# Block-by-block output projection, longer zero products, and a last expert whose result is added half by half, in an fp32 encoder kernel

## The chip, the cores and the metric

The kernel runs on one core of a Trainium2 chip. The metric is the device time in microseconds (us) of one execution; a median of several executions is given. Engines are called PE (TensorE, matrix products), DVE (VectorE), ACT (ScalarE), POOL (GpSimd) and SP (SyncE, which here only issues transfers). "bank" is a region of PSUM in which PE accumulates, 128 partitions by 512 numbers.

## The reference

Two layers over 256 tokens of width 1024, in float32: an even one and an odd one, each with a token mixer and a channel mixer.

```python
for i in range(DEPTH):                      # DEPTH = 2
    hn = rms_norm(h, norm_mix[i])
    if i % 2 == 0:  mix = fourier_mixer(hn, fourier_w_in[j], fourier_w_out[j])
    else:           mix = neighbourhood_attention(hn, nat_w_qkv[j], nat_rpb[j], nat_w_o[j])
    h = h + mix
    hn = rms_norm(h, norm_ffn[i])
    if i % 2 == 0:  ff = swiglu(hn, ffn_w_gate[j], ffn_w_up[j], ffn_w_down[j])
    else:           ff = moe_swiglu(hn, router_w[j], router_b[j], expert_w_gate[j], expert_w_up[j], expert_w_down[j])
    h = h + ff
return rms_norm(h, final_norm)
```

The Fourier mixer multiplies by `w_in`, takes the real part of a 2-D transform over tokens and over groups of 256 channels, and multiplies by `w_out`. `moe_swiglu` forms 8 logits for each token, sends the token to the two experts with the highest, weights their results by a softmax over the two, and adds. An expert is `(silu(x @ w_gate) * (x @ w_up)) @ w_down` with a hidden width of 3584. `rms_norm` multiplies by a gain vector per channel.

## The kernel before, in words

**Precision.** Every large product is three matmuls (`three`, L1250 to L1252): of each fp32 operand a high half `..._hi` (a rounding copy, made by ACT) and a rest `..._lo` (whole less high half, made by DVE) are kept, and high by high, high by low and low by high are added in one bank. Products of three that the profile names by these lines are all of this kind.

**Weights.** All weights come in pieces of 1 MiB (128 partitions by 2048 numbers, four 512-wide rows of one K tile each). SP loads them into seven slots `raw`; ACT makes `w_hi` (L458), DVE `w_lo` (L753), in three slots. `split_past(n)` in ACT's and in DVE's code makes all the pieces up to n + 3 that aren't made yet. PE's `ready` waits for a piece's `w_lo`; the last matmul on a piece frees its slot (`piece_used`). The very first weight piece is split in parts of 512 columns (L470, L761), and so is the second.

**Order.** No scheduler is at work: each engine's program is written out by hand, and an instruction that waits holds up all that stand behind it on its engine. The 256 tokens are two blocks b of 128, the 1024 channels two halves q (or c) of 512.

**Start.** PE first runs `still(12)`, twelve products of zeros (L1321, two trace records each), then `first_projection` (L1272: eight K tiles, each with its wait for a part of `w_lo`), the second half of `w_in`, and then `token_dft` and `channel_dft` for the Fourier mixer, in pairs of banks `T[m % 2]` and `Y[g % 2]`: product m waits until DVE is done with product m - 2 (`pt_lo_done`). `stream_second` (L1307) lets PE wait for `act_lo` of a new activation in two steps of two quarters.

**Output projection and router.** `wo_product(c, half, b)` multiplies by half of the attention's output matrix for column half c and token block b. DVE adds a result to h (`add_projection`, L797). PE transposes h (`transpose_stream(3, ...)`, L1297), ACT and DVE scale it by the norm's gain and halve it (L504, L778), PE multiplies with the router's weights `rw_parts` (`logits_hi` L1578, `logits_lo` L1585), and DVE finds the best two experts in a chain of small operations (L1013 to L1030, its result `used`). PE then ranks the tokens of each expert (L1610 to L1614), DVE makes a selection matrix `sel` (L1074), and PE gathers the first expert's tokens by products with it (L1619), transposes them (L1655) and starts the first expert. Between these waits PE runs `keep_warm(6)` and `keep_warm(2)`, products of an identity matrix that nobody reads (L1592; below they are called zero products too). `token_hi`, `token_lo` halve h for the gather. `split_past(W0 + n)` counts from the output projection's first piece; a piece is halved past it as soon as ACT and DVE come to that call.

**Experts.** For each expert PE runs, for seven steps c of 512 hidden columns, gate, up and, one step later, down (`down(c, half)`), the last one adding in the banks Y. The last expert, `LAST`, isn't handled by a loop: `result_hi` and `result_rest` halve its result, four pairs of products with `selT` (L1766, L1767) scatter it back to token order, and `add_result` (L1111) adds it to h. `gate_weights` (L1133) forms the two softmax weights, six small DVE operations in step 1 of that expert. ACT then squares the rows of h (L494), POOL makes 1/sqrt (L444, L446), DVE scales (L1236), and SP stores four parts of 256 KB (L392).

## Time and profile before

| | us |
|---|---|
| median of three executions | 1366.86 |
| lowest, highest | 1364.64, 1367.56 |
| the profiled execution | 1367.15 |
| its span in the trace | 1365.3 |

The span runs from the first to the last instruction in the trace; 1.85 us of the profiled execution lie outside it. The granted clock of PE was 0.992 on average. In the rows below, a line of the timeline gives start, duration, engine, source line, operation, result and operands, the number of records, and in square brackets how long the engine had been idle and what ended that. Consecutive matmuls overlap in the trace: the time of one is the distance of two starts, not its duration. A line of windows gives, for a stretch, its length, the busy time with the number of records, the granted clock (1.00 is full), the busy share of the transfer engines and GB/s.

### The profile page before, as it was taken

How to read it: one execution, taken by the hardware profiler on the slowest of the kernel's cores; microseconds unless marked ns; L12 is line 12 of the kernel's file. 1: busy time of each engine (PE TensorE's matmuls, PEld its weight loads, DVE VectorE, ACT ScalarE, POOL GpSimd, SP SyncE). 2: the span in 40 equal slices, each digit the busy share in tenths (PEclk: the TensorE clock that was granted, in tenths of full speed). 3: DMA queues.
4: the chain of work that ended last, by engine and by line, in shares of the span. 5: the costliest groups of instructions: out<-in, count | busy, mean ns of one | idle time of the engine just before them, and what ended most of it. 6: DMA issues, size and time to landing. Idle time of an engine off the chain costs nothing.

```text
span 1365.3 us, 17406 instructions
## 1 busy us (share of the span) xinstructions
PE 1344.7 (98%) x6341; PEld 1117.9 (82%) x6341; DVE 1111.9 (81%) x815; ACT 923.2 (68%) x755; POOL 34.5 (3%) x48
## 2 busy tenths in 40 slices
PE   8999999999999999999999999999999999999997
PEld 7888888787878888888888888888888888888885
DVE  5756666655678889888988988898898889889997
ACT  6554444545647778777777877877787787777774
POOL 0000000000101000000000000000000000002000
PEclk8999999999989999999999999999999999999999
DMA  9666775563339999999999999999999999999992
GB/s 354 246 207 179 210 211 190 175 204 104 101 109 378 383 378 365 395 382 357 398 388 372 373 394 377 358 398 388 368 376 394 367 370 397 381 374 385 396 394 90
DMA packets 194971, 432.32 MB, mean 317 GB/s; under 512 B 19632, under 2 KB 22064, under 8 KB 194800
## 3 DMA queue, kind: packets, MB, share of 16 engines
q1 hardware_dynamic: 178784, 416.28, 83.4%
q0 software_dynamic: 3360, 11.78, 2.2%
q10 hardware_dynamic: 12784, 3.69, 1.8%
q8 instruction: 27, 0.44, 0.1%
q14 instruction: 16, 0.13, 0.0%
HBM read 425.94 MB, written 5.78 MB: 316 GB/s over the span
## 4 chain that ended last, share of the span: by engine, by line
PE 95%; DVE 3%; ACT 1%; issue 1%; DMA 0%; POOL 0%; DVEq 0%; ACTq 0%
PE bank_G L1250 10%; PE bank_G L1252 10%; PE bank_G L1251 10%; PE bank_U L1250 10%; PE bank_U L1252 10%; PE bank_U L1251 10%; PE bank_Y L1250 8%; PE bank_Y L1252 8%; PE bank_Y L1251 8%; PE bank_T L1696 2%; PE bank_T L1250 1%; PE bank_T L1252 1%; PE bank_T L1251 1%; DVE w_lo L753 1%; PE bank_G L1512 0%
## 5 line engine op out<-in xcount | busy, mean ns | idle before, releaser
L753 DVE TENSOR_TENSOR w_lo<-raw,w_hi 128x2048 fp32r<-128x2048 f32 x390 | 885.9, 2289 | 184.6 <-ACT w_hi L458 183.8
L458 ACT ACTIVATE w_hi<-raw 128x2048 fp32r<-128x2048 f32 x390 | 748.6, 1920 | 276.6 <-PE bank_U L1252 98.2
L1250 PE MATMUL bank_Y<-w_hi,hidT_hi 128*128 128x512 f32 x492 | 192.2, 391 | 0.0
L1252 PE MATMUL bank_Y<-w_hi,hidT_lo 128*128 128x512 f32 x492 | 191.6, 389 | 0.0
L1251 PE MATMUL bank_Y<-w_lo,hidT_hi 128*128 128x512 f32 x492 | 191.5, 389 | 0.0
L1250 PE MATMUL bank_U<-w_hi,xg_hi 128*128 128x512 f32 x448 | 179.1, 400 | 0.0
L1250 PE MATMUL bank_G<-w_hi,xg_hi 128*128 128x512 f32 x448 | 175.2, 391 | 1.3 <-DVE xg_lo L774 0.9
L1252 PE MATMUL bank_U<-w_hi,xg_lo 128*128 128x512 f32 x448 | 175.0, 391 | 0.0
L1251 PE MATMUL bank_U<-w_lo,xg_hi 128*128 128x512 f32 x448 | 174.5, 390 | 0.0
L1252 PE MATMUL bank_G<-w_hi,xg_lo 128*128 128x512 f32 x448 | 174.5, 390 | 0.0
L1251 PE MATMUL bank_G<-w_lo,xg_hi 128*128 128x512 f32 x448 | 174.4, 389 | 0.0
L1252 PEld LDWEIGHTS bank_Y<-w_hi,hidT_lo 128*128 128x128 f32 x492 | 92.4, 188 | 19.4
L1250 PEld LDWEIGHTS bank_Y<-w_hi,hidT_hi 128*128 128x128 f32 x492 | 92.3, 188 | 19.3
L1251 PEld LDWEIGHTS bank_Y<-w_lo,hidT_hi 128*128 128x128 f32 x492 | 92.4, 188 | 18.7
L1250 PEld LDWEIGHTS bank_G<-w_hi,xg_hi 128*128 128x128 f32 x448 | 84.1, 188 | 21.0 <-issue 2.9
L1252 PEld LDWEIGHTS bank_U<-w_hi,xg_lo 128*128 128x128 f32 x448 | 84.1, 188 | 18.3
L1252 PEld LDWEIGHTS bank_G<-w_hi,xg_lo 128*128 128x128 f32 x448 | 84.1, 188 | 17.7
L1251 PEld LDWEIGHTS bank_G<-w_lo,xg_hi 128*128 128x128 f32 x448 | 84.1, 188 | 17.1
L1251 PEld LDWEIGHTS bank_U<-w_lo,xg_hi 128*128 128x128 f32 x448 | 84.3, 188 | 16.3
L1250 PEld LDWEIGHTS bank_U<-w_hi,xg_hi 128*128 128x128 f32 x448 | 84.2, 188 | 15.9
L1250 PE MATMUL bank_G<-w_hi,act_hi 128*128 128x512 f32 (+1 forms) x176 | 68.6, 390 | 4.4 <-DVE w_lo L761 3.1
L1250 PE MATMUL bank_U<-w_hi,act_hi 128*128 128x512 f32 (+1 forms) x176 | 67.7, 384 | 0.3 <-DVE act_lo L774 0.3
(301 smaller groups left out, 1363.5 us busy)
## 6 DMA issues: line engine op xcount, KB each, us to landing
raw<-in_expert_w_gate SPq DMA_DIRECT2D x112, 1024.0 KB, 7.7
raw<-in_expert_w_up SPq DMA_DIRECT2D x112, 1024.0 KB, 7.8
raw<-in_expert_w_down SPq DMA_DIRECT2D x112, 1024.0 KB, 7.7
raw<-in_nat_w_qkv SPq DMA_DIRECT2D x12, 1024.0 KB, 5.1
raw<-in_ffn_w_gate SPq DMA_DIRECT2D x11, 1024.0 KB, 8.9
raw<-in_ffn_w_up SPq DMA_DIRECT2D x11, 1024.0 KB, 5.7
raw<-in_ffn_w_down SPq DMA_DIRECT2D x11, 1024.0 KB, 5.2
raw<-in_fourier_w_out SPq DMA_DIRECT2D x4, 1024.0 KB, 15.6
```

Of the source, the lines that this page charges most:

```text
L458: nc.scalar.activation(w_hi[w][:], raw[s][:], ACT.Copy).then_inc(hi_made, 1)
L753: nc.vector.tensor_tensor(w_lo[w][:], raw[s][:], w_hi[w][:].bitcast(f32), ALU.subtract).then_inc(lo_made, 1)
L1250: nc.tensor.matmul(out_, xh, wh, start=start, stop=False)
L1251: nc.tensor.matmul(out_, xh, wl, start=False, stop=False)
L1252: return nc.tensor.matmul(out_, xl, wh, start=False, stop=stop)
L1696: last = nc.tensor.transpose(T[c % 2][:, P * k:P * (k + 1)], hid[c % 2][:, P * k:P * (k + 1)], ident[:])
```

## The change

1. `still(23)` stands for `still(12)`; `token_dft` and `channel_dft` go round four banks each (`BY_TOKEN`, `BY_CHANNEL`), so product m waits for product m - 4, and the wait for `ft_channels` is gone.
2. `project(..., stream=i)` waits for `act_lo` before every second K tile, one quarter at a time.
3. The output projection ends block by block: (c 0, b 0), (c 1, b 0), transposes of block 0, logits of block 0, then those of block 1. The norm's gain is multiplied into the router's weights (`rw`, once, on DVE), so the halves of the tokens are plain copies of a whole bank. Square sums, 1/rms, `rest` and `logit` are made for each block as it comes. `keep_warm(24)` and `keep_warm(8)` stand for 6 and 2. The call `split_past(W0 + 3)` is gone on both ACT and DVE, and its piece is halved at the next such call.
4. `gates` (three small DVE operations) stay in step 1 of the last expert; the other three, `gate_weights`, stand in step 6.
5. The last expert's last two pieces are used column half by column half (`last_columns`): all of half 0, two K tiles of half 1, `scatter(0)`, the last two K tiles of half 1, `scatter(1)`. The last piece is halved in two column halves; DVE adds a half's result before it comes to the other half's rest; squares are taken by halves; for channel half 1 DVE multiplies by the gain ahead of 1/rms and ACT scales.

The core of the diff:

```diff
+    TOKENS = [G, [U[1], Y[1]]]
     PARTS = PIECE // BANK
...
+    BY_TOKEN = [T[0], T[1], G[0], G[1]]
+    BY_CHANNEL = [Y[0], Y[1], U[0], U[1]]
...
-                sp.wait_ge(fin_done, 2 * b + q + 1)
+                sp.wait_ge((fin_done, fin_scaled)[q], b + 1)
...
         split_past(W0 + 1)
-        act.wait_ge(s_rout, 64)
+        act.wait_ge(rw_scaled, 1)
         nc.scalar.activation(mo["rw_parts"][:, :, :NE], mo["rw"][:], ACT.Copy).then_inc(rw_hi_done, 1)
-        split_past(W0 + 3)
-        stream_hi(3, 0)
...
+        def tokens_hi(b, half):
+            act.wait_ge(tr_done, 4 * 2 + 2 * b + half + 1)
+            nc.scalar.activation(act_hi[:, 4 * half:4 * half + 4, P * b:P * (b + 1)], four(TOKENS[b][half]), ACT.Copy).then_inc(act_hi_done, 1)
...
+        split_past(W0 + 2)
+        squares_of_half(0)
+        token_hi(0, 0)
+        tokens_hi(0, 0)
+        token_hi(0, 1)
+        tokens_hi(0, 1)
+        squares_of_half(1)
+        tokens_hi(1, 0)
+        token_hi(1, 0)
+        tokens_hi(1, 1)
+        token_hi(1, 1)
         split_past(W0 + 4)
         act.wait_ge(gap_done, 1)
...
+                    (split_hi_by_halves if kept and j + SPLIT == PER_EXPERT - 1 else split_hi)(j + SPLIT, E)
...
+            act.wait_ge(e_added, 2 * NB * (NE + 1))
+        for q in range(2):
+            for b in range(NB):
+                act.wait_ge(e_added, NB * q + b + 1)
+                cs = slice(BANK * q, BANK * (q + 1))
+                total = sumsq[:, 4, b:b + 1] if q else mo["sumsq_half"][:, b:b + 1]
+                nc.scalar.activation(mo["hn_hi"][:, b, cs], h[:, b, cs], ACT.Square, accum_out=total).then_inc(fin_sq, 1)
+        for b in range(NB):
+            act.wait_ge(fin_gain, b + 1)
+            act.wait_ge(fin_rstd, b + 1)
+            nc.scalar.activation(hn[:, b, BANK:], hn[:, b, BANK:], ACT.Copy, scale=rstd[:, 4, b:b + 1]).then_inc(fin_scaled, 1)
...
-        split_past(W0 + 2)
-        add_projection(at["wo"], ao_psum, WO[0], 0)
-        split_past(W0 + 3)
-        stream_lo(3, 0)
-        token_lo(0, 0)
-        token_lo(0, 1)
-        dve.wait_ge(s_rout, 64)
-        nc.vector.tensor_copy(mo["token"][:].rearrange("p b n -> p (b n)"), mo["count"][:, S:S + 2 * NB]).then_inc(token_made, 1)
-        nc.vector.tensor_copy(mo["before_h"][:], mo["before"][:]).then_inc(before_done, 1)
...
-        dve.wait_ge(h_half, 6)
...
+            part = h[:, b, BANK * c:BANK * (c + 1)]
+            nc.vector.tensor_tensor(part, WO[c][b][:], part, ALU.add).then_inc(h_half, 1)
+        def tokens_lo(b, half):
+            dve.wait_ge(act_hi_done, 4 * 3 + 2 * b + half + 1)
+            rest(act_lo[:, 4 * half:4 * half + 4, P * b:P * (b + 1)], four(TOKENS[b][half]),
+                 act_hi[:, 4 * half:4 * half + 4, P * b:P * (b + 1)]).then_inc(act_lo_done, 1)
+        def squares_of_rest(b):
...
+        dve.wait_ge(s_rout, 64)
+        nc.vector.tensor_tensor(mo["rw"][:], mo["rw"][:], gains[:, 3].unsqueeze(2).to_broadcast([P, KD, NE]), ALU.mult).then_inc(rw_scaled, 1)
+        dve.wait_ge(rw_hi_done, 1)
+        rest(mo["rw_parts"][:, :, NE:], mo["rw"][:], mo["rw_parts"][:, :, :NE]).then_inc(rw_lo_done, 1)
+        nc.vector.tensor_copy(mo["token"][:].rearrange("p b n -> p (b n)"), mo["count"][:, S:S + 2 * NB]).then_inc(token_made, 1)
+        nc.vector.tensor_copy(mo["before_h"][:], mo["before"][:]).then_inc(before_done, 1)
+        nc.vector.tensor_scalar(mo["below"][:], mo["count"][:, 0:NE], -float(NE), None, ALU.add).then_inc(before_done, 1)
+        split_past(W0 + 1)
+        add_wo(0, 0)
+        split_past(W0 + 2)
+        add_wo(0, 1)
+        squares_of_rest(0)
+        tokens_lo(0, 0)
+        token_lo(0, 0)
+        add_wo(1, 0)
+        tokens_lo(0, 1)
+        token_lo(0, 1)
+        tokens_lo(1, 0)
+        add_wo(1, 1)
+        squares_of_rest(1)
+        tokens_lo(1, 1)
         dve.wait_ge(before_done, 2)
         full = [P, NB, NE]
...
         for b in range(NB):
+            dve.wait_ge(rstd_done, 3 + b + 1)
+            dve.wait_ge(logit_psum, b + 1)
...
-                for q in range(2):
+                result_rest(E, q)
+                for b in range(NB):
                     dve.wait_ge(e_scatter, NB * (2 * (E - LAST) + q) + b + 1)
+                    dve.wait_ge(terms_added, 4 * NB)
                     part = h[:, b, BANK * q:BANK * (q + 1)]
                     src = T[q] if b == 0 else (G, U)[q][1]
-                    last = nc.vector.scalar_tensor_tensor(out=part, in0=src[:], scalar=mo["weight"][:, b, bass.ds(e, 1)],
-                                                          in1=part, op0=ALU.mult, op1=ALU.add)
...
+        def gate_weights():
             link(nc.vector.tensor_tensor(mo["first"][:], mo["first"][:], each_token(mo["g1"][:]), ALU.mult))
             link(nc.vector.tensor_tensor(mo["second"][:], mo["second"][:], each_token(mo["g2"][:]), ALU.mult))
...
-                        gate_weights()
+                        gates()
...
+                if (kind, c, half) == ("up", STEPS - 1, 0) and kept and not sweep:
+                    gate_weights()
...
-                    (result_rest if kept else result_copy)(E)
+                    (results(E, e) if kept else result_copy(E))
                 if ahead or j + SPLIT < PER_EXPERT:
-                    split_lo(j + SPLIT, E)
+                    (split_lo_by_halves if kept and j + SPLIT == PER_EXPERT - 1 else split_lo)(j + SPLIT, E)
...
+        dve.wait_ge(e_added, 2 * NB)
+        second = slice(BANK, D)
+        for b in range(NB):
+            nc.vector.tensor_tensor(hn[:, b, second], h[:, b, second], mo["gain"][:, 1, second], ALU.mult).then_inc(fin_gain, 1)
         for b in range(NB):
             dve.wait_ge(fin_rstd, b + 1)
-            for q in range(2):
-                cs = slice(BANK * q, BANK * (q + 1))
-                nc.vector.scalar_tensor_tensor(out=hn[:, b, cs], in0=h[:, b, cs], scalar=rstd[:, 4, b:b + 1],
-                                               in1=mo["gain"][:, 1, cs], op0=ALU.mult, op1=ALU.mult).then_inc(fin_done, 1)
+            nc.vector.scalar_tensor_tensor(out=hn[:, b, :BANK], in0=h[:, b, :BANK], scalar=rstd[:, 4, b:b + 1],
+                                           in1=mo["gain"][:, 1, :BANK], op0=ALU.mult, op1=ALU.mult).then_inc(fin_done, 1)
     @block.tensor
...
+                        if stream is not None and b == 0 and kk % 2 == 0:
+                            pe.wait_ge(act_lo_done, 4 * stream + kk // 2 + 1)
...
             def before(n, b):
-                if (n, b) == (0, 0):
-                    pe.wait_ge(act_lo_done, 4 * i + 2)
...
-                if (n, b) == (1, 0):
-                    pe.wait_ge(act_lo_done, 4 * i + 4)
...
-        still(12)
+        still(23)
...
-            if m >= 2:
-                pe.wait_ge(pt_lo_done, m - 1)
+            if m >= 4:
+                pe.wait_ge(pt_lo_done, m - 3)
...
             pe.wait_ge(pt_lo_done, 2 * g + 2)
-            if g >= 2:
...
+            for k in range(KH):
+                if k == KH // 2:
+                    transpose_tokens_of(1, 0)
+                kk = KH + k
+                last = three(WO[1][1][:], act_hi[:, kk, P:], act_lo[:, kk, P:], wh[:, k], wl[:, k], False, kk == KD - 1)
...
+        wo_product(0, 1, 0)
+        wo_product(1, 1, 0)
+        transpose_tokens_of(0, 0)
+        wo_product(0, 1, 1)
+        transpose_tokens_of(0, 1)
+        last_wo_product()
         pe.wait_ge(rw_lo_done, 1)
-        pe.wait_ge(act_lo_done, 4 * 3 + 2)
-        for q in range(2):
-            logits_hi(q)
-            logits_lo(q)
-        transpose_stream(3, 1)
-        logits_hi(2)
-        logits_hi(3)
-        logits_lo(2)
-        logits_lo(3).then_inc(logit_psum, 1)
-        keep_warm(6)
+        logits(0, 0)
+        logits(0, 1)
+        transpose_tokens_of(1, 1)
+        logits(1, 0)
+        logits(1, 1)
+        keep_warm(24)
...
-        keep_warm(2)
+        keep_warm(8)
...
+            def last_columns(q, rows, first=0):
...
+                    j = AT["down", c, half]
+                    if q == 0 and half and k == 0:
+                        pe.wait_ge(lo_half, E - LAST + 1)
+                    if q == 1 and half and k == 0:
...
+                last_columns(0, 4)
+                last_columns(1, 2)
+                scatter(0)
+                last_columns(1, 2, 2)
+            else:
+                down(STEPS - 1, 0)
+                down(STEPS - 1, 1)
...
                 first_gate(E + 1)
-            if not kept:
-                return
-            pe.wait_ge(e_selT_copy, E - LAST + 1)
-            for q in range(2):
-                pe.wait_ge(e_ylo, 2 * (E - LAST) + 1 + q)
...
+            if kept:
+                scatter(1)
```

On DVE, from the output projection to the first expert (names with their buffer numbers). Before:

```order
L753 TENSOR_TENSOR w_lo0<-raw1,w_hi0 128x2048
L797 TENSOR_TENSOR h<-bank_U0,h 128x512
L797 TENSOR_TENSOR h<-bank_Y0,h 128x512
L753 TENSOR_TENSOR w_lo1<-raw2,w_hi1 128x2048
L778 SCALAR_TENSOR_TENSOR act_lo<-bank_G0,gains,act_hi 128x256 x2
...
L774 TENSOR_TENSOR xg_lo_62<-bank_U1,xg_hi_61 128x512
L1201 TENSOR_REDUCE most_96<-bank_T1 128x1
L753 TENSOR_TENSOR w_lo2<-raw3,w_hi2 128x2048
L1205 SCALAR_TENSOR_TENSOR hn<-h,rstd,gain_58 128x1024 x2
L753 TENSOR_TENSOR w_lo0<-raw4,w_hi0 128x2048
```

After the change (L794 is the split, L1031 the sum with h):

```order
L1031 TENSOR_TENSOR h<-bank_U0,h 128x512
L794 TENSOR_TENSOR w_lo0<-raw1,w_hi0 128x2048
L1031 TENSOR_TENSOR h<-bank_T0,h 128x512
L1044 ISA xg_65,sumsq<-h,sumsq_half_72 128x512
...
L822 TENSOR_TENSOR xg_lo_62<-bank_U1,xg_hi_61 128x512
L1268 TENSOR_REDUCE most_96<-bank_T1 128x1
L794 TENSOR_TENSOR w_lo1<-raw2,w_hi1 128x2048
L794 TENSOR_TENSOR w_lo2<-raw3,w_hi2 128x2048
L1272 SCALAR_TENSOR_TENSOR hn<-h,rstd,gain_58 128x1024 x2
L794 TENSOR_TENSOR w_lo0<-raw4,w_hi0 128x2048
```

The third split ahead of the first expert's second up piece, `w_lo1<-raw2`, stood in the output projection and now stands behind `most`, with `w_lo2<-raw3`, the two `hn` and `w_lo0<-raw4` behind it.

On PE, from the last logits to the gather. Before:

```order
L1585 MATMUL bank_G0<-rw_parts_69,act_lo 128x8
L1585 MATMUL bank_G1<-rw_parts_69,act_lo 128x8
L1592 MATMUL bank_T0<-ident 128x128 x6
L1610 MATMUL bank_T1<-used_88,before_h_79 128x8
L1611 MATMUL bank_T1<-used_88,before_h_79 128x8
L1612 MATMUL bank_T1<-used_88,ones_78 128x8
L1613 MATMUL bank_T1<-used_88,ones_78 128x8
L1614 MATMUL bank_T1<-used_88,ones_78 128x8
L1592 MATMUL bank_T0<-ident 128x128 x2
L1619 MATMUL bank_G1<-hn_hi_59,sel_66 128x512 x2
```

After the change (L1656 is `keep_warm`):

```order
L1639 MATMUL bank_Y1<-ident,h 128x128 x4
L1646 MATMUL bank_G1<-rw_parts_69,act_hi 128x16 x4
L1648 MATMUL bank_G1<-rw_parts_69,act_lo 128x8 x4
L1646 MATMUL bank_G1<-rw_parts_69,act_hi 128x16 x4
L1648 MATMUL bank_G1<-rw_parts_69,act_lo 128x8 x4
L1656 MATMUL bank_T0<-ident 128x128 x24
L1688 MATMUL bank_T1<-used_88,before_h_79 128x8
...
L1656 MATMUL bank_T0<-ident 128x128 x8
L1697 MATMUL bank_G1<-hn_hi_59,sel_66 128x512 x2
```

Only the transposes and logits of half a block stand behind the last sum of h now, and 24 and 8 zero products stand where 6 and 2 stood.

On PE, at the end of the last expert. Before:

```order
L1250 MATMUL bank_Y0<-w_hi2,hidT_hi0 128x512
L1251 MATMUL bank_Y0<-w_lo2,hidT_hi0 128x512
L1252 MATMUL bank_Y0<-w_hi2,hidT_lo0 128x512
L1250 MATMUL bank_Y1<-w_hi2,hidT_hi0 128x512
L1251 MATMUL bank_Y1<-w_lo2,hidT_hi0 128x512
L1252 MATMUL bank_Y1<-w_hi2,hidT_lo0 128x512
L1250 MATMUL bank_Y1<-w_hi2,hidT_hi0 128x512
L1251 MATMUL bank_Y1<-w_lo2,hidT_hi0 128x512
L1252 MATMUL bank_Y1<-w_hi2,hidT_lo0 128x512
L1766 MATMUL bank_T0<-y_hi_63,selT_67 128x512
L1767 MATMUL bank_T0<-y_lo_64,selT_67 128x512
L1766 MATMUL bank_G1<-y_hi_63,selT_67 128x512
```

After the change (L1829, L1830 are the scatter):

```order
L1320 MATMUL bank_Y1<-w_lo1,hidT_hi0 128x512
L1321 MATMUL bank_Y1<-w_hi1,hidT_lo0 128x512
L1829 MATMUL bank_T0<-y_hi_63,selT_67 128x512
L1830 MATMUL bank_T0<-y_lo_64,selT_67 128x512
L1829 MATMUL bank_G1<-y_hi_63,selT_67 128x512
L1830 MATMUL bank_G1<-y_lo_64,selT_67 128x512
L1319 MATMUL bank_Y1<-w_hi2,hidT_hi0 128x512
L1320 MATMUL bank_Y1<-w_lo2,hidT_hi0 128x512
L1321 MATMUL bank_Y1<-w_hi2,hidT_lo0 128x512
L1319 MATMUL bank_Y1<-w_hi2,hidT_hi0 128x512
```

The four products that scatter the first half of the result now stand ahead of the last six products of the second half (four of them shown).

## Rows read from the trace of the kernel before

**Rows 1.** Page: busy time, share, instructions of each engine.

```profile
PE 1344.7 (98%) x6341; PEld 1117.9 (82%) x6341; DVE 1111.9 (81%) x815; ACT 923.2 (68%) x755; POOL 34.5 (3%) x48
```

**Rows 2.** Waits of PE, whole span: us in total, times, longest.

```profile
PE bank_T L1250 <- DVE pt_lo L774: 0.7, 1, 0.7
...
PE bank_G L1250 <- DVE w_lo L753: 0.4, 1, 0.4
```

**Rows 3.** Source line 1321, zero products: ns min/median/max, first, last start.

```profile
L1321 PE MATMUL bank_U<-hid x24: 274/421/580, 1.1 to 5.3; 128*128 128x128 f32 x24
```

**Rows 4.** Windows of the start: us, PE busy (records), PEclk, DMA, GB/s.

```profile
5.60:8.60 3.00, 0.00 (x0) 0.86 0.97 376
...
9.60:11.60 2.00, 2.00 (x6) 0.50 1.06 399
...
14.60:16.60 2.00, 2.00 (x10) 1.00 0.99 407
```

**Rows 5.** Timeline, first projection on PE and DVE: start, us, instruction.

```profile
8.65 0.77 PE L1250 MATMUL bank_G<-w_hi,act_hi 128*128 128x512 f32 x1 [3.08 <-DVE w_lo L761]
15.53 1.28 DVE L761 TENSOR_TENSOR w_lo<-raw,w_hi 128x512 fp32r<-128x512 f32 x2
17.58 2.29 DVE L753 TENSOR_TENSOR w_lo<-raw,w_hi 128x2048 fp32r<-128x2048 f32 x1 [0.77 <-ACT w_hi L458]
23.27 2.29 DVE L753 TENSOR_TENSOR w_lo<-raw,w_hi 128x2048 fp32r<-128x2048 f32 x1 [3.40 <-ACT w_hi L458]
...
33.28 0.28 PE L1250 MATMUL bank_T<-dft_hi,u_hi 128*128 128x256 f32 x1
```

**Rows 6.** Timeline, DVE and PE ahead of the q, k, v projection.

```profile
256.56 1.65 DVE L778 SCALAR_TENSOR_TENSOR act_lo<-bank_T,gains,act_hi 128x256 fp32r<-128x256 f32 x4
...
258.36 0.47 PE L1250 MATMUL bank_G<-w_hi,act_hi 128*128 128x512 f32 x1 [1.36 <-DVE act_lo L778]
```

**Rows 7.** Windows of the router stage: us, PE busy (records), PEclk.

```profile
390.00:393.00 3.00, 3.00 (x16) 0.51 0.00 0
400.30:401.10 0.80, 0.80 (x5) 1.00 0.00 0
```

**Rows 8.** Timeline, PE in the router stage.

```profile
393.09 2.91 PE L1592 MATMUL bank_T<-ident 128*128 128x128 f32 x12
396.62 0.19 PE L1610 MATMUL bank_T<-used,before_h 128*128 128x8 bf16 x1 [0.63 <-DVE used L1029]
...
398.17 1.22 PE L1619 MATMUL bank_G<-hn_hi,sel 128*128 128x512 f32 x2 [0.19 <-DVE sel L1074]
...
403.58 0.47 PE L1250 MATMUL bank_G<-w_hi,xg_hi 128*128 128x512 f32 x1 [0.90 <-DVE xg_lo L774]
...
409.10 0.39 PE L1250 MATMUL bank_U<-w_hi,xg_hi 128*128 128x512 f32 x1
```

**Rows 9.** Timeline, DVE in the router stage.

```profile
381.27 2.29 DVE L753 TENSOR_TENSOR w_lo<-raw,w_hi 128x2048 fp32r<-128x2048 f32 x1 [1.25 <-ACT w_hi L458]
...
396.39 0.17 DVE L1029 TENSOR_TENSOR used<-first,second 128x16 bf16<-128x16 f32 x1
...
404.14 2.29 DVE L753 TENSOR_TENSOR w_lo<-raw,w_hi 128x2048 fp32r<-128x2048 f32 x1
406.35 2.47 DVE L1205 SCALAR_TENSOR_TENSOR hn<-h,rstd,gain 128x1024 f32<-128x1024 f32 x2
408.75 2.28 DVE L753 TENSOR_TENSOR w_lo<-raw,w_hi 128x2048 fp32r<-128x2048 f32 x1
```

**Rows 10.** Timeline, end of the last expert and of the program.

```profile
1345.53 0.60 PE L1696 MATMUL bank_T<-ident,hid 128*128 128x128 f32 x4
...
1354.36 0.60 ACT L698 ACTIVATE y_hi<-bank_Y 128x512 fp32r<-128x512 f32 x1 [0.76 <-PE bank_Y L1252]
...
1355.73 0.50 PE L1766 MATMUL bank_T<-y_hi,selT 128*128 128x512 f32 x1
```

**Rows 11.** Window of the output's transfer: us, busy, PEclk, DMA share, GB/s.

```profile
1362.00:1364.00 2.00, 0.00 (x0) 0.00 (x0) 0.73 (x2) 0.00 (x0) 0.00 (x0) 0.50 1.00 380
```

196 lines of the change are left out of this document (111 added, 85 removed).

## The prediction

> **What bounds the kernel now.** I read the busy shares first: PE is busy for 1344.7 of 1365.3 us [rows 1]. It can win no more than the 20.6 us in which it is idle, plus what it loses at half clock. The list of PE's waits and the timeline around each came next. None of the waits lies in the seven experts that run unchanged, so the change is decided in four short places: the start, the hand-over to the q, k, v projection, the router stage, and the last expert with the program's end. There the reader should see what PE waits for, and whether the granted clock is full.
>
> At the start PE runs twelve zero products until 5.6 us, then waits 3.1 us for the first part of `w_lo` [rows 5]; the clock falls in that gap and stays at half until after 13.6 us [rows 4]. In the router stage it falls again: 0.51 between 390 and 393, full at 400.3 [rows 7]. All my durations are of this execution, 1367.15 us, 0.3 above the median of the three.
>
> **The start.** Twelve products are 24 records with starts from 1.1 to 5.3 [rows 3]. A record at half clock costs (2.91 - 0.56) / 11 = 0.2135 us by the twelve in the router stage [rows 8], whose last alone takes 0.56 (an estimate from the longest of its kind), so 0.107 at full clock. With 23 distances in 4.2 us, the first 16 were slow and 7 fast. 46 records then end at 1.1 + 16 x 0.2135 + 30 x 0.107 = 7.7 us. The first weight product still starts at 8.65, since DVE's part is no earlier, but the gap is 0.9 us and not 3.1, and I expect the clock to stay full. The 96 products up to the Fourier stage took 33.28 - 8.65 = 24.6 us [rows 5]; at full clock, 0.227 each (24 take 409.10 - 403.58 = 5.5 us [rows 8]), they would take 21.8. They can't all come earlier: the last piece's `w_lo` is ready at 23.27 + 2.29 = 25.56 [rows 5], because ACT splits it only behind the norm's square sums, and 24 products follow it, to 31.1. That is 2.2 us earlier. In the Fourier stage two waits for `pt_lo`, 0.7 us each [rows 2], can go with four banks; but DVE's splits stand in the same row and aren't earlier, so DVE comes last there and I carry only 2.1 us through. **Term: -2.1.** Bounds: the clock's fall and rise came at a moment of this execution; with a fall in the gap as before only the banks' gain is left, at least 0.8; with a fast first projection and one bank wait more, -2.4.
>
> Here a rule of the Trainium skill bears ("TensorE: Matmul & The Clock Gate", What's actually happening): throttled is the default, activity releases the clock, and the point of release differs between executions. Rows 3 and 4 agree: full records come only after some microseconds of zero products, and full clock returns only amid the projection. By the page the term is this or nearly nothing, by execution; my bounds say the same without it.
>
> **Waits by pairs of K tiles.** The q, k, v projection waits till 258.36 for all four quarters of `act_lo`, made in one stretch of 1.65 us from 256.56 [rows 6]. One quarter would do: two of them are ready at about 257.4, so PE starts 0.8 earlier and then runs 6 products (1.4 us) to each 0.4 of DVE. **Term: -0.8** (0 to -0.9). The gate projection showed no wait.
>
> **Router stage.** The last sum of h is followed only by the transposes, copies, rests and eight logit products of half a block, where before two blocks' halves and sixteen products at half clock followed. By the durations of the rows in this stage I put the end of the logits at 390.5 instead of 393.1, and `used`, 3.3 us behind them before (393.09 to 396.39 + 0.17 [rows 8, 9]), at 393.4, as block 0's `rest` and `logit` are made by then. That would win 3 us. But 24 zero products stand in front of the rank product. 48 records take 5.1 us at full clock and 10.2 at half. The clock has fallen by 390 in this stage; I let it rise within the dense zero products as it did at the start, after 16 slow records: 16 x 0.2135 + 32 x 0.107 = 6.9 us, to 397.4. PE then waits for nothing: `used` has been ready for 4 us, and the gain is gone. The rank product comes 0.8 later than at 396.62 [rows 8]. Eight products (16 records, 1.7 us) follow, DVE's `sel` takes 1.5 (396.62 to 398.17); the gather starts at 399.25. From there it was 403.58 - 398.17 = 5.4 us to the first expert product, four products of it at half clock; at full clock 0.8 less. So 403.85: **term +0.25.** If the clock never falls, the zero products end at 395.6 and it is -1.5; if it never rises in them, they end at 400.7, and the eight behind them and the gather are slow too: +6.2.
>
> The removed `split_past(W0 + 3)` costs more. Its `w_lo`, 2.2 us of DVE at 381.27, lay beside PE's products [rows 9]. It now stands behind `xg_lo` and `most`, ahead of the split at 404.14, the two `hn` (2.4) and the split at 408.75, all of which it delays by 2.2. That last split was ready at 411.0 and is needed by the second up piece, 36 products behind the first: 403.58 + 5.5 + 12 x 0.227 = 411.8. It will be ready at 413.2 by the old clock: PE waits 1.4, and 0.1 for the moved piece itself, needed 2.7 us after the first product and ready about 2.8 after. Nothing recovers this, as PE has no idle time in the experts. **Term: +1.5** (0.8, if DVE's `hn` or ACT's split of the same piece slip into gaps, to 1.7).
>
> **Last expert.** Moving three small DVE operations, 0.2 each like `used` [rows 9], out of step 1 frees the one wait there, 0.4 by the list [rows 2], 0.6 with the refill of PE's pipeline. They reappear ahead of the last `hid`, behind which PE transposes at 1345.53 without a wait and without slack [rows 10]: +0.5. **Term: -0.1** (-0.6 to +0.1).
>
> **The end.** `scatter(0)`, four products of 0.23 and a refill, about 1.0 to 1.2 us, now runs before the last six products of half 1. Before, it ran while ACT and DVE made half 1's `y_hi` and `y_lo` (1354.36 to 1355.7 [rows 10]), where PE had nothing else. All of half 1's chain is later by it: `y_hi`, `y_lo`, `scatter(1)`, the sums. The square sum that closes is over 512 columns instead of 1024 and takes 0.4 less (an estimate from the 0.60 of a copy of 512 columns [rows 10]). So 1/rms and the first output part come 0.7 later. The output moves at 380 GB/s [rows 11], 1.05 MB in 2.75 us: later parts that are ready sooner gain nothing. **Term: +0.7** (-0.2, if the sums made early also clear DVE, to +0.9).
>
> **Sum.** -2.1 - 0.8 + 0.25 + 1.5 - 0.1 + 0.7 = -0.55, that is 1366.6 against 1367.15. Against the median, 1366.3; I take 1366.5 between. Half a microsecond can't be told from no change: a measurement of this kernel tells about 0.2%, 2.7 us.
>
> **Rivals.**
> *The clock stays full in the router stage.* For it: PE idles there only in gaps under 1 us, like those of [rows 8], and the new order has denser work. Against: it fell at 390 in spite of that. The gather's and the zero products' share gives -1.75: 1364.8. The Trainium skill's rule ("TensorE: Matmul & The Clock Gate", Why this matters for your kernels) asks only that no long idle gap stand between matmuls; by it the clock would stay full here, and the sum is this rival's. Rows 7 speak against it. Chance 0.15.
> *The parts pay as meant.* The clock stays full and the moved split meets slack (DVE reaches it during the gather's products, which are long enough), and the end costs nothing: -0.55 - 1.75 - 1.5 - 0.4 = -4.2, 1362.6. Against: on DVE the split stands behind `xg_lo`, which is what PE's first expert product waits for. Chance 0.17.
> *The clock falls at the start all the same.* The 3.1 us gap is closed, but the first products are spaced by DVE's parts. Then the start gives -0.8: 1367.8. Chance 0.13.
> *Slower: zero products at half clock.* Once PE has begun them it can't leave. If the clock stays down, 24 cost 10.2 us and not 6.9, the eight 3.4, and the stage is up to 6 us later, 1372.5; from about 8.5 us for the 24 on, with the moved split, the total is slower by over 0.2%. For it: the clock was at half for 10 us in this stage, zero products included [rows 7, 8]. Against: there they were only six, with gaps. A middle case gives 1370. Chance 0.13.
>
> **How the numbers follow.** The forecast has 0.42. Faster by over 0.2%, below 1364.1: 0.17 and a third of the first rival, with some of the forecast's lower edge, 0.25. Slower, above 1369.6: 0.13 and an edge of 0.02, 0.15. Within: 0.60. The range leaves out 0.1 on either side: down to the case where the parts pay, 1362.5; up to the middle case of the slow one, 1369.7.
>
> **What would show it.** Right: the first weight product near 8.65 and no clock below full until the router stage; the Fourier stage's start near 31.1; no PE wait for `used`, with the zero products ending 2 us or more after it; a new PE wait for `w_lo` of over 1 us in the first expert's second up piece; PE waits ahead of the last `hidden_transposes`; the first output issue at about 0.7 us later relative to the last `hidT_lo`. Wrong: PE waiting for `used` again, no wait in the first expert, or a start no shorter than before.

## The result and the profile after the change

The changed kernel takes 1369.62 us (median of 11 executions, 1368.17 to 1370.65), the kernel before 1366.25 us (11 executions on the same chip, 1364.64 to 1368.03). The ratio is 1.0023, with a 95% interval of 1.0016 to 1.0031: slower by 0.23%, 3.4 us by the medians. The profiled execution took 1370.04 us with a span of 1368.2 us, 2.9 longer than the span before. Below, "relative to" a point means counted from that point in each profile, so that shifts of earlier stages drop out.

The columns of all timelines are those of the rows before. First PE's waits in the whole span (engine, operation waited in, what ended it: us in total, times, longest). [rows 2] and the first row of [rows 5] answer to it:

```profile
PE bank_T L1829 <- DVE y_lo L822: 1.5, 1, 1.5
...
PE bank_U L1319 <- DVE w_lo L794: 1.0, 1, 1.0
...
PE bank_G L1319 <- DVE act_lo L826: 0.6, 1, 0.6
PE bank_G L1646 <- DVE act_lo L822: 0.5, 1, 0.5
```

The wait of 3.1 us at the start and the one for `used` are gone. The two largest new ones are 1.5 us ahead of the last scatter (L1829), and 1.0 us for the `w_lo` of the moved split's neighbours (L794). The two waits for `pt_lo` that the four banks were to free are still there, 0.8 and 0.5 us (0.7 each before). PE is busy for 1349.9 us (before 1344.7 [rows 1]) and the program ends later, so PE is busy longer without need: with products that nobody needs, or at half clock. The start:

```profile
1.10 8.35 PE L1388 MATMUL bank_U<-hid 128*128 128x128 f32 x46 [1.10 <-POOL hid L412]
9.64 0.47 PE L1319 MATMUL bank_G<-w_hi,act_hi 128*128 128x512 f32 x1 [0.19 <-DVE w_lo L809]
...
31.70 0.28 PE L1319 MATMUL bank_T<-dft_hi,u_hi 128*128 128x256 f32 x1
...
44.98 0.40 PE L1319 MATMUL bank_G<-w_hi,act_hi 128*128 128x512 f32 x1
```

PE in the router stage (answering to [rows 8]), from the last logits to the first expert product:

```profile
387.05 1.02 PE L1646 MATMUL bank_G<-rw_parts,act_hi 128*128 128x16 f32 x4 [0.52 <-DVE act_lo L822]
387.93 0.99 PE L1648 MATMUL bank_G<-rw_parts,act_lo 128*128 128x8 f32 x4
388.78 7.62 PE L1656 MATMUL bank_T<-ident 128*128 128x128 f32 x48
396.24 0.17 PE L1688 MATMUL bank_T<-used,before_h 128*128 128x8 bf16 x1
...
398.15 0.71 PE L1697 MATMUL bank_G<-hn_hi,sel 128*128 128x512 f32 x2
...
402.58 0.47 PE L1319 MATMUL bank_G<-w_hi,xg_hi 128*128 128x512 f32 x1 [0.90 <-DVE xg_lo L822]
```

Windows of the same stretch (us, PE busy with records, granted clock, transfers), and DVE's `used` and what came next on it. [rows 7] and [rows 9] stood here before:

```profile
386.00:388.00 2.00, 1.48 (x9) 0.55 0.00 0
388.00:390.00 2.00, 2.00 (x11) 0.50 0.00 0
390.00:392.00 2.00, 2.00 (x11) 0.50 0.00 0
392.00:394.00 2.00, 2.00 (x15) 0.75 0.00 0
394.00:396.00 2.00, 2.00 (x20) 1.00 0.00 0
```

```profile
391.85 0.17 DVE L1094 TENSOR_TENSOR used<-first,second 128x16 bf16<-128x16 f32 x1
396.61 0.17 DVE L1101 SCALAR_TENSOR_TENSOR slot<-bank_T,used 128x16 f32<-128x16 f32 x1 [4.51 <-issue]
```

`used` was there at 392.0, and the product that needs it started at 396.24. Behind the gather, DVE (answering to the last three rows of [rows 9]) and the product that waited:

```profile
403.14 4.49 DVE L794 TENSOR_TENSOR w_lo<-raw,w_hi 128x2048 fp32r<-128x2048 f32 x2
407.56 2.47 DVE L1272 SCALAR_TENSOR_TENSOR hn<-h,rstd,gain 128x1024 f32<-128x1024 f32 x2
409.95 2.28 DVE L794 TENSOR_TENSOR w_lo<-raw,w_hi 128x2048 fp32r<-128x2048 f32 x1
```

```profile
412.29 0.50 PE L1319 MATMUL bank_U<-w_hi,xg_hi 128*128 128x512 f32 x1 [1.04 <-DVE w_lo L794]
```

The program's end, PE and DVE (L1183 adds a result to h, L1302 is the multiplication by the gain, L1305 the scaling by both), then POOL's last 1/rms steps and SP's output. [rows 10] answers to it:

```profile
1355.64 0.39 PE L1321 MATMUL bank_Y<-w_hi,hidT_lo 128*128 128x512 f32 x1
1357.53 0.47 PE L1829 MATMUL bank_T<-y_hi,selT 128*128 128x512 f32 x1 [1.50 <-DVE y_lo L822]
...
1358.30 0.40 PE L1830 MATMUL bank_U<-y_lo,selT 128*128 128x512 f32 x1
```

```profile
1358.94 0.74 DVE L1183 SCALAR_TENSOR_TENSOR h<-bank_U,weight,h 128x512 f32<-128x512 f32 x1
1361.71 1.29 DVE L1302 TENSOR_TENSOR hn<-h,gain 128x512 f32<-128x512 f32 x2 [2.03 <-issue]
1362.92 1.41 DVE L1305 SCALAR_TENSOR_TENSOR hn<-h,rstd,gain 128x512 f32<-128x512 f32 x2
```

```profile
1360.30 0.57 POOL L461 TENSOR_TENSOR rstd<-rstd,half_power 128x1 f32<-128x1 f32 x1
```

```profile
1363.70 1.83 SPq L400 DMA_DIRECT2D out<-hn  x4
```

The same stretch before:

```profile
1356.53 0.39 PE L1767 MATMUL bank_U<-y_lo,selT 128*128 128x512 f32 x1
```

```profile
1357.83 0.74 DVE L1118 SCALAR_TENSOR_TENSOR h<-bank_U,weight,h 128x512 f32<-128x512 f32 x1
```

```profile
1359.98 2.74 DVE L1236 SCALAR_TENSOR_TENSOR hn<-h,rstd,gain 128x512 f32<-128x512 f32 x4 [1.42 <-POOL rstd L446]
```

```profile
1360.12 1.03 POOL L446 TENSOR_TENSOR rstd<-rstd,half_power 128x1 f32<-128x1 f32 x1
```

```profile
1360.77 2.32 SPq L392 DMA_DIRECT2D out<-hn  x4
```

Between fixed points of the two profiles the 2.9 us split up as follows. "w_out" is the first product of the Fourier mixer's output weights, "last hid" the last transposes of the last expert (1345.53 before [rows 10]).

| stretch | before | after | difference | forecast |
|---|---|---|---|---|
| start to w_out | 46.80 | 44.98 | -1.82 | -2.1 |
| w_out to the q, k, v projection's first product | 211.56 | 210.76 | -0.80 | -0.8 |
| from there to the first expert product | 145.22 | 146.84 | +1.62 | +0.25 |
| to that expert's first transposes of hid | 16.57 | 18.14 | +1.57 | +1.5 |
| to last hid | 925.38 | 925.13 | -0.25 | -0.1 |
| last hid to the end of the span | 19.77 | 22.35 | +2.58 | +0.7 |
| sum | 1365.3 | 1368.2 | +2.9 | -0.55 |

### The profile page after: what moved, and what is told of

Same layout as the page of the kernel before. It is cut to its first block, busy times and chain, and to the rows that moved or that the text cites. A ratio compares the mean times of both kernels' runs of the same rounds, so it can differ in the third digit from the quotient of the medians.

```text
span 1368.2 us, 17556 instructions
## 1 busy us (share of the span) xinstructions
PE 1349.9 (99%) x6411; PEld 1123.6 (82%) x6411; DVE 1111.1 (81%) x813; ACT 924.0 (68%) x758; POOL 32.2 (2%) x51
## 4 chain that ended last, share of the span: by engine, by line
PE 93%; DVE 3%; DMA 1%; ACT 1%; issue 1%; SPq 0%; POOL 0%; DVEq 0%; ACTq 0%
PE bank_U L1319 10%; PE bank_G L1319 10%; PE bank_U L1321 10%; PE bank_U L1320 10%; PE bank_G L1321 10%; PE bank_G L1320 10%; PE bank_Y L1319 8%; PE bank_Y L1321 8%; PE bank_Y L1320 8%; PE bank_T L1774 2%; DVE w_lo L794 1%; DMA raw<-in_fourier_w_in 1%; PE bank_T L1321 1%; PE bank_T L1319 1%; PE bank_T L1320 1%
## 5 line engine op out<-in xcount | busy, mean ns | idle before, releaser
L794 DVE TENSOR_TENSOR w_lo<-raw,w_hi 128x2048 fp32r<-128x2048 f32 x389 | 883.5, 2288 | 182.3 <-ACT w_hi L473 181.5
```

The costliest lines, as they stand in the source:

```text
L794: nc.vector.tensor_tensor(w_lo[w][:], raw[s][:], w_hi[w][:].bitcast(f32), ALU.subtract).then_inc(lo_made, 1)
```

## The experiments

Every kernel below was timed in five rounds beside the kernel before, whose medians lie between 1366.28 and 1366.68 us. Several differences are near what a profile of one execution varies by: w_out stood at 46.80, 46.71 and 45.98 in three profiles of kernels that start like the one before. So medians carry the verdicts, and profiles the mechanism.

The medians need care too, because the executions of one kernel lie in two loose groups, the longer with the lower mean granted clock. Of the changed kernel three took 1368.2 to 1369.0 us (mean clock 0.995 to 0.996) and eight 1369.3 to 1370.7 (0.994 to 0.995). In a kernel where most executions fall into the lower group the median is a microsecond or so better by that alone. All ratios below are to the kernel before.

### Zero products: fewer in the changed kernel

```diff
-        keep_warm(24)
+        keep_warm(8)
...
-        keep_warm(8)
+        keep_warm(4)
```

> The changed kernel with 8 and 4 zero products in place of 24 and 8. Theory (the zero products hold the rank product back: `used` was ready at 392.0 and the rank product ran at 396.24): 16 records at half clock end at about 392.2, the rank product follows at once, and the first expert product comes about 4 us earlier than at 402.6 after the same start; total about 4 us below the changed kernel, near 1365.5. Rival 1 (the long run of zero products is what brings the clock back, so that without it the gather runs at half clock): only 3 us, or less, with windows of 0.5 after 394. Rival 2 (DVE's or ACT's splits ahead of the first expert come last instead): first expert product unchanged, total unchanged.

1365.06 us, ratio 0.9993 (0.9984 to 1.0002): 4.6 us less than the changed kernel. Its router stage:

```profile
387.54 3.21 PE L1656 MATMUL bank_T<-ident 128*128 128x128 f32 x16
390.85 0.19 PE L1688 MATMUL bank_T<-used,before_h 128*128 128x8 bf16 x1
...
391.01 1.40 PE L1656 MATMUL bank_T<-ident 128*128 128x128 f32 x8
392.21 0.73 PE L1697 MATMUL bank_G<-hn_hi,sel 128*128 128x512 f32 x2
...
396.66 0.47 PE L1319 MATMUL bank_G<-w_hi,xg_hi 128*128 128x512 f32 x1 [0.90 <-DVE xg_lo L822]
```

The first product pairs of the gather take the same 0.7 us as with 24 and 8 (0.73 and 0.71), and the first expert product comes 5.9 us earlier, 5.5 of it in the stretch from w_out. Some 0.8 of that is not the edit's: in this profile the last logits still ran at full clock (0.61 and 0.59 us for four pieces; 1.02 and 0.99 in the changed kernel's), so that 4.6 by the medians is nearer to the price. So 8 and 4 restore the clock as well as 24 and 8, and all the others are time that the path pays.

### No zero products at all

The starting point is the kernel "with four steps undone" below; `keep_warm(8)` and `keep_warm(4)` are taken out of it.

```diff
-        keep_warm(8)
...
-        keep_warm(4)
```

> The kernel c1 (8 and 4 zero products) with none at all in the router stage. Theory A (zero products buy full clock for the gather and the first expert products): clock at half from about 388 until after the gather, gather and first products 1.0 to 2.5 us longer, total 1 to 2.5 above c1. Theory B (they buy nothing, since the clock rises in the gather by itself): first expert product within 0.5 us, total as c1. In both the rank product follows `used` within 0.2 us.

1363.71 us (0.9981, 0.9972 to 0.9990), 1.2 us slower than its starting point by the medians, though the two intervals overlap (0.9962 to 0.9983 there). The trace shows why: PE now waits 3.2 us for `used` and 1.1 for `sel`, the gather's first three pairs take 1.22, 1.06 and 1.06 us where they took 0.73, 0.62 and 0.62, and the stretch from w_out to the first expert product is 354.25 us against 352.24. So the products seem worth having; their number was wrong.

### The same zero products in the old order

```diff
-        keep_warm(6)
+        keep_warm(24)
...
-        keep_warm(2)
+        keep_warm(8)
```

> The kernel before with one edit, its zero products ahead of rank and gather at 24 and 8 in place of 8 and 4. Theory: the price comes with the products themselves, whatever the order ahead of them: rank's product starts near 400 us in place of 396.6, the gather's products run 0.8 to 1 us faster at the full clock, and the time is 2 to 3 us up, 1369. Rival: the price exists only with the new order, whose last logits ran at half clock; then the 24 are done at the full clock before the counts are ready, and the time is within 0.5 us of the kernel before.

The edit goes from 6 and 2 to 24 and 8; the kernel before never had the 8 and 4 that the expectation names. 1369.97 us (1.0023, 1.0013 to 1.0032), 3.3 us slower than the kernel before, and as slow as the changed one. Its zero products and the rank product:

```profile
392.98 7.36 PE L1592 MATMUL bank_T<-ident 128*128 128x128 f32 x48
400.17 0.17 PE L1610 MATMUL bank_T<-used,before_h 128*128 128x8 bf16 x1
...
402.09 0.71 PE L1619 MATMUL bank_G<-hn_hi,sel 128*128 128x512 f32 x2
```

Rank comes at 400.17 and not at 396.62 [rows 8], the gather gives 1.0 back (4.4 us and not 5.4 to the first expert product). The price comes with the products themselves and needs no new order. The stretch from w_out to the first expert product was 359.81 us here, 357.60 in the changed kernel: the new order with its waits by pairs was worth 2.2 us even under 24 products. With 8 and 4 it was 352.13, against 356.78 in the kernel before with its 6 and 2: 4.65 less. Both differences are of single profiles; among six profiles of the new order with 24 and 8 this stretch lay between 356.36 and 358.05.

### The moved split

Its neighbours on DVE in another order: the two splits ahead of the two `hn`.

```diff
+        for j in range(SPLIT, AHEAD):
+            split_lo(j, 0)
...
-        for j in range(SPLIT, AHEAD):
-            split_lo(j, 0)
```

> The changed kernel with one swap on DVE ahead of the first expert: the split for the second up piece stands before the two hn operations, not behind them. Theory (PE's 1.57 us in the first up come from the moved split, which pushes this one to 412.2): its split is ready at 409.9, before it is needed at 410.8, PE's wait for w_lo there is gone, total 1.5 us below the changed kernel. Rival (the wait only moves: the hn rows are stored for the next experts' gather and come 2.3 us later): the wait in the first up is gone and another of about the same size appears later in the first or second expert; total unchanged.

1369.39 us (1.0020, 1.0011 to 1.0030), 0.2 less than the changed kernel. The wait moved on to the next gate's products and kept 0.6 of its 1.0 us. The fourth split behind the gather ended at 414.5 in both kernels: four splits and two `hn` are one row without a gap, whatever their order. My theory, that only the order was bad, fell: it is the length of the row. Next, DVE's half of the moved split between `used` and the slots, where DVE had 4.5 us of nothing:

```diff
         dve.wait_ge(used_done, 1)
+        split_past(W0 + 3)
         dve.wait_ge(rank_psum, 1)
```

> The changed kernel with the moved split's DVE half put between `used` and the rank's `slot`, where DVE waits 4.5 us for PE's zero products. Theory (what the moved split costs is 2.2 us more DVE work behind the gather, in whatever order it stands there, since swapping the split with hn only moved PE's wait): DVE does it in its idle time, both waits of PE for w_lo (second up, and next gate) are gone, from the first expert product to the first hidden transposes 17.6 us less 1.5, total 1.5 below the changed kernel. Rival (the wait in the first expert has its cause in ACT's halves or in the loads): it stays, total unchanged.

1368.08 us (1.0014, 1.0005 to 1.0023), 1.5 less. The stretch from the first expert product to the transposes of hid is 16.61 us (before 16.57, changed 18.14), and no PE wait for `w_lo` is left. So this term is the split's place in DVE's row, and neither ACT's halves nor the loads.

### The end

The final scaling as before:

```diff
-        for b in range(NB):
-            nc.vector.tensor_tensor(hn[:, b, second], h[:, b, second], mo["gain"][:, 1, second], ALU.mult).then_inc(fin_gain, 1)
...
+            for q in range(2):
+                nc.vector.scalar_tensor_tensor(out=hn[:, b, cs], in0=h[:, b, cs], scalar=rstd[:, 4, b:b + 1],
+                                               in1=mo["gain"][:, 1, cs], op0=ALU.mult, op1=ALU.mult).then_inc(fin_done, 1)
```

> The changed kernel with the final scaling as in the kernel before: DVE scales all four parts by 1/rms and gain, no products with the gain ahead, ACT not used. Theory A (the two products with the gain stand between the sums and the first scaled part on DVE): the first output part is issued about 1.2 us earlier after the last sum (4.0 us before, 2.8 then), total 1.2 below. Theory B (DVE waits 2.0 us after its last sum for the code behind the branch, whatever stands there): first scaling starts 2.0 us after the last sum, no earlier; A and B can both hold. Rival (the output's transfer is the bound, and four parts on DVE alone come no faster): total unchanged.

1367.47 us (1.0013, 1.0004 to 1.0022), 2.15 less. The tail from last hid is 21.17 us, 1.18 less; about 1 us of the 2.15 is not in the tail. The router stage holds it, by luck and not by the edit: with the same code there, the zero products ended at 394.93 and not at 396.24, as the clock fell later and came back earlier (windows as above; there the changed kernel has 0.55, 0.50, 0.50 and 0.75):

```profile
386.00:388.00 2.00, 1.38 (x12) 1.00 0.00 0
388.00:390.00 2.00, 2.00 (x12) 0.60 0.00 0
390.00:392.00 2.00, 2.00 (x12) 0.55 0.00 0
392.00:394.00 2.00, 2.00 (x20) 1.00 0.00 0
```

Of this kernel's eleven executions eight lie in the lower group (1366.9 to 1367.8, mean clock 0.996 to 0.997) and three in the upper (1368.6 to 1369.3, 0.995). By the means of the groups it is 1.3 and 1.1 us under the changed kernel, which is the tail's 1.18.

`scatter(0)` behind all columns, the sums behind both rests:

```diff
-                last_columns(1, 2)
+                last_columns(1, 4)
...
-                last_columns(1, 2, 2)
...
+            for q in range(2):
```

> The changed kernel with the scatter of half 0 behind all products of the last down, as before the change, and DVE making both rests before the sums. Theory (the four products ahead of the last six delay half 1's chain by 1.2 to 1.5 us, since they fill no gap there): y_hi of half 1 starts 0.25 us after the last down product, which comes 1.3 us earlier; last sum 0.7 to 1.3 us earlier, total about 1 us below the changed kernel. Rival (the sums on DVE, four times 0.67 us, then come in one row and give it back): last sum at the same distance from the last hidden transposes, total unchanged.

1367.30 us (1.0011, 1.0002 to 1.0020), 2.3 less; tail 21.27 us, 1.08 less. Again the median gives about 1 us more than the tail, and again it fell into the lower group: seven executions took 1366.9 to 1367.7 and four 1368.3 to 1369.3, which is 1.4 and 1.3 us under the changed kernel by the means of the groups. Relative to last hid, PE's last products and the last scatter are 1.3 earlier and DVE's last sum 1.0. One thing is common to both runs (first row: final scaling as before; second row: scatter behind):

```profile
1360.35 2.74 DVE L1299 SCALAR_TENSOR_TENSOR hn<-h,rstd,gain 128x512 f32<-128x512 f32 x4 [1.98 <-POOL rstd L461]
1361.01 1.29 DVE L1303 TENSOR_TENSOR hn<-h,gain 128x512 f32<-128x512 f32 x2 [1.94 <-issue]
```

In both, DVE idles 1.9 to 2.0 us between the last sum and its next operation. For the second the trace knows no releaser; for the first it names 1/rms, but that had been ready since 1359.56, 0.8 us. Between the last sum and the next operation stands the jump over the second sweep's code (`over`), which is taken. In the kernel before, too, the first scaling starts 0.6 us after its 1/rms is ready (1359.38). The next kernel is the one before with that code in the arm that falls through, and once more behind the sweep:

```diff
+        with dve.If(over < 1):
+            final_scaling()
```

> The kernel before the change, with DVE's final scaling put twice: once in a branch that is taken by falling through (no second sweep) and once behind the second sweep. The same operations run. Theory (DVE begins the final scaling about 3.0 us after PE's last scatter product, by the code behind the jump over the second sweep, while 1/rms of block 0 is ready 0.6 us earlier): the first scaled part starts 0.1 to 0.2 us after 1/rms, 0.5 us earlier than before, and total 0.4 below the kernel before. Rival (DVE waited for 1/rms, as the trace names it): same distance of 0.6 us, total unchanged or later by the jump that now stands at the end.

```profile
1359.30 1.41 DVE L1222 SCALAR_TENSOR_TENSOR hn<-h,rstd,gain 128x512 f32<-128x512 f32 x2 [0.85 <-POOL rstd L446]
1361.16 1.41 DVE L1222 SCALAR_TENSOR_TENSOR hn<-h,rstd,gain 128x512 f32<-128x512 f32 x2 [0.45 <-POOL rstd L446]
```

The scaling now starts 0.04 after 1/rms. The theory of the jump holds for the start, but the time is 1367.53 us (1.0008, 0.9999 to 1.0017), no gain: the second pair waits for block 1's 1/rms, which POOL finished at 1361.13 while DVE was at the first pair, so that DVE's last scaling ended 17.19 us after last hid in both kernels. So the jump's 0.6 us was cover for POOL's second 1/rms. The tail is 20.12 us against 19.77; the 0.35 more stand behind DVE's last operation and are not explained.

### The start

The changed kernel with 12 zero products again:

```diff
-        still(23)
+        still(12)
```

> The changed kernel with 12 zero products at the start, as before the change. Theory (the 23 close the gap before the first weight product and so keep the clock full through the first projection): PE idles 3 us before 8.6 us, granted clock 0.5 for some microseconds of the first projection, the Fourier stage starts about 2 us later (33.3 against 31.0 to 31.7), total 1 to 2 us above the changed kernel. Rival (the first projection is paced by DVE's and ACT's splits anyway): Fourier stage at 31.0 to 31.7 and total unchanged.

1369.92 us (1.0025, 1.0016 to 1.0034): 0.3 more than the changed kernel, within what the two medians vary by. PE waited 2.8 us again, the clock was at 0.58 between 9.6 and 11.6, and yet the Fourier stage began at 31.62 (changed kernel 31.70). The half clock lasted less long here than in the kernel before, where it still stood at 0.50 between 11.6 and 13.6; here it was 1.00 there. That differs between executions: with 12 zero products the Fourier stage began at 33.28, 33.20, 33.21, 31.86 and 31.62 in five profiles. Then the two edits of the start in the kernel before, alone and together:

```diff
-        still(12)
+        still(23)
```

> The kernel before with 23 zero products at its start instead of 12, nothing else. Theory (the forecast's start term: the clock stays full in the first projection and all later work comes earlier): Fourier stage at about 31.1 instead of 33.3, w_out at 45.0 to 45.5 instead of 46.8, total 1.3 to 2 us below the kernel before. Rival (DVE and ACT pace the Fourier stage, as 12 zero products in the changed kernel cost it only 0.3 us): Fourier stage earlier, but w_out by less than 0.7, total within 0.7 us of the kernel before.

```diff
+    BY_TOKEN = [T[0], T[1], G[0], G[1]]
+    BY_CHANNEL = [Y[0], Y[1], U[0], U[1]]
...
-            if m >= 2:
-                pe.wait_ge(pt_lo_done, m - 1)
+            if m >= 4:
+                pe.wait_ge(pt_lo_done, m - 3)
```

> The kernel before with the Fourier stage over four banks each, nothing else. Theory (the two bank waits of 0.7 us and their successors are what the start won): w_out 0.7 to 1.5 us earlier after the Fourier stage's start (13.5 us before), total 0.7 to 1.5 below the kernel before. Rival (DVE is last there, so banks give nothing): 13.5 us as before, total unchanged.

> The kernel before with both edits of its start, the zero products in the first wait at 23 in place of 12 and the first products over four banks. Theory of the records: the two together bring the first output weights' product from 46.80 to about 45.0 us, and the time is 1.0 to 1.8 us down, 1364.8 to 1365.6. Rival from the runs with each alone (0.0 and -0.9 us): the Fourier stage goes at the pace of VectorE and ScalarE, so both together give what the banks give, 0.5 to 1.0 us: 1365.6 to 1366.1.

| kernel before with | median, us | difference | ratio (95%) | Fourier stage from, w_out at |
|---|---|---|---|---|
| 23 zero products | 1366.62 | 0.0 | 0.9999 (0.9990 to 1.0008) | 31.27, 45.77 |
| four banks | 1365.77 | -0.9 | 0.9995 (0.9986 to 1.0004) | 33.21, 45.96 |
| both | 1365.09 | -1.6 | 0.9989 (0.9980 to 0.9998) | 31.14, 44.80 |

With full clock alone the Fourier stage starts 2 us earlier and then takes 14.5 us (before 13.5), with a wait for `pt_lo` of 1.7 us; with four banks alone it starts late and takes 12.75. Both together are worth 1.6 us and are the only ones of the three whose interval excludes no change. That they are worth more together than the sum of each alone (0.9) is not shown, as the intervals are wider than the difference. How much the zero products carry stays open: taken out of the changed kernel they cost 0.3 and not 0.7.

### Four steps undone, and two more edits

The changed kernel with zero products 8 and 4, the final scaling and the scatter as before, and `gate_weights` right ahead of the last results. Beside the diffs above:

```diff
-                if (kind, c, half) == ("up", STEPS - 1, 0) and kept and not sweep:
-                    gate_weights()
...
+                    if kept and not sweep:
+                        gate_weights()
```

> The changed kernel with four of its parts altered together: 8 and 4 zero products, final scaling on DVE as before, scatter of half 0 behind the last down products as before, and the three small gate_weights operations right ahead of the result's rests. Theory (the costs found one by one add): 4.6 + 1.2 + 1.1 + 0.4 = 7.3 us below the changed kernel, 1362.3, 0.3% below the kernel before. Rival (the gains overlap: the first two share the same wait for the code behind the jump, or the start's gain varies): 1364 or more.

1362.52 us (0.9972, 0.9962 to 0.9983), 7.1 less than the changed kernel and within 0.3 of what was expected. The medians of the single edits alone would have given 9 us (4.6, 2.15 and 2.3): what the two edits of the end had beside their tails goes with the group their medians fell into. The tail is 19.74 us, as before the change; the wait ahead of the last hid is gone; the wait for `w_lo` (1.1 us) is left. Further edits on top of it: block 1's last transposes ahead of block 0's last logits, the moved split in parts (half behind block 0's logits, a quarter between the two `xg_lo`, the last behind them), and the changed kernel's final scaling in the arm that falls through.

```diff
-        logits(0, 1)
         transpose_tokens_of(1, 1)
+        logits(0, 1)
...
+            if b == 0:
+                moved_lo(0, 2)
...
+        moved_lo(2, 3)
...
+        moved_lo(3, 4)
```

> The kernel c1 with three more edits: the last transposes ahead of the logits of block 0's second half; the moved split in parts, half of it between block 0's and block 1's logits and a quarter between the gathered tokens' copies; the changed kernel's final scaling (gain first, ACT for half 1), but reached on DVE by falling through. Theory: 0.6 from the transposes, 1.2 to 1.5 from PE's wait for the split in the first expert, 0.4 at the end since the gain is multiplied while 1/rms is made: 2.3 us below c1, near 1360.2. Rival (each of the small parts put in a gap delays the chain of small operations by what it takes): first expert product 0.5 to 1 us later than in c1, total within 1 us of c1.

1361.96 us (0.9970, 0.9958 to 0.9982; six executions), 0.6 less than with four steps undone, 1.8 more than expected. The expert's stretch is 16.61, as it should be, but the tail is 21.14 and not 19.74. DVE and POOL there:

```profile
1351.28 1.29 DVE L1313 TENSOR_TENSOR hn<-h,gain 128x512 f32<-128x512 f32 x2
1353.31 0.77 DVE L1316 SCALAR_TENSOR_TENSOR hn<-h,rstd,gain 128x512 f32<-128x512 f32 x1 [0.74 <-POOL rstd L462]
1354.52 0.75 DVE L1316 SCALAR_TENSOR_TENSOR hn<-h,rstd,gain 128x512 f32<-128x512 f32 x1 [0.45 <-POOL rstd L462]
```

```profile
1351.50 1.11 POOL L460 TENSOR_SCALAR rstd<-sumsq,sumsq_half 128x1 f32<-128x1 f32 x1 [0.50 <-ACT hn_hi L782]
```

DVE's multiplications now start 0.04 us after its last sum ends, where 2.03 us lay between in the changed kernel: the wait at the jump is gone here too. But POOL's step takes 0.27 us in the changed kernel and 1.11 here, and it ends when DVE's multiplications by the gain do (1352.6). With the old end in their place:

> The kernel with four steps undone, and with two of the three further edits: the transposes ahead of the router's last logits, and the moved split in parts (half behind block 0's logits, a quarter between the gathered rows' two copies, the last quarter behind them). The final scaling stands as before. Theory: those two edits gave their 1.7 us up to the last hidden transposes, and the new end took 1.4 us of it back, so with the old end the time is 1.7 us under the kernel with four steps undone: 1360.8, with the tail from the last hidden transposes to the span's end again at 19.7. Rival: the last expert's end waits for something that does not move with the hidden transposes; then it is within 0.5 us of 1362.5.

1360.61 us (0.9956, 0.9942 to 0.9970; five executions): 1.9 less than with four steps undone, tail 19.75. It is the fastest of all, 6.1 us under the kernel before and 9.0 under the changed one. The forecast of 1360.8 held, the rival didn't. The expert's stretch gives 1.5 of the 1.9 (16.65 against 18.14); what the transposes gave can't be told from it, as the stretch from w_out to the first expert product was 352.98 us here, 351.69 in the run before and 352.24 with four steps undone.

## Why the prediction was wrong, and where it was right

The time fell into the range (1362.5 to 1369.7), at its upper edge, but the forecast was no measurable change, and the kernel is slower by 0.23%. The profiles miss the sum by 3.45 us: 1.9 at the end, 1.4 in the router stage, 0.3 at the start, the rest in small terms. Two terms were mis-sized, and both on work that I had priced as hidden or short.

**The router term (+0.25, measured +1.62).** The reading that `used` would be ready long ahead and that PE "can't leave" the zero products was right: 4.2 us between 392.0 and 396.24, no PE wait for `used`. The step that failed is the end of the logits. I put it 2.6 us earlier; it came 1.7 earlier (393.09 - 388.78, less the 2.62 that the stages ahead had won), because the clock had fallen before block 1's last logits (1.02 and 0.99 us for four pieces, where those at full clock took 0.59). In the run with 8 and 4 zero products, where the clock had not fallen yet, these logits took 0.8 us less. The second step that failed is the price of the zero products: 7.46 us instead of 6.9, about (7.46 - 48 x 0.107) / 0.1065 = 22 slow records, not 16. I had taken the 16 from one stretch of one execution; in five other profiles of the same code the 24 took 7.1 to 8.3 us, at the longest near the 8.5 from which I had counted the slower rival. The 24 products in the old order show that the price, 3.3 us, is the products' own. What I didn't ask is whether fewer would do, although "`used` has been ready for 4 us" already said that most of them were waste.

The rule of the Trainium skill ("TensorE: Matmul & The Clock Gate", Why this matters for your kernels), by which only a long idle gap takes the clock down, was a rival here. The windows after the change speak against it: 0.55 between 386 and 388 with idle gaps of no more than 0.6 us. By it the time would have been 1364.8.

**The end (+0.7, measured +2.58).** The step "So 1/rms and the first output part come 0.7 later" failed. Relative to last hid, block 0's 1/rms came 1.2 later and the first output part 2.6, because 1/rms did not set the end. Worked out from the rows, in three pieces:

- Last hid to the end of the last sum: 13.04 before, 13.83 after, +0.79. `scatter(0)` ahead of six products makes the last scatter product end 1.46 later (12.85 after last hid, before 11.39), more than the 1.0 to 1.2 that I put there, and one sum fewer behind it gives 0.67 back; PE waits 1.5 us for half 1's `y_lo` with nothing left to do. The run with it undone: -1.08.
- End of the last sum to DVE's next operation: 1.41 before, 2.03 after, +0.62. In the old code three sums still ran behind the last scatter products or beside them, and I take it that they hid part of the jump; in the new one only two do, and they start when the scatter ends. Counted from the end of PE's last scatter product, it is nearly the same in both: 1359.98 - 1356.92 = 3.06 and 1361.71 - 1358.70 = 3.01.
- DVE's first operation to the first store: 0.79 before, 1.99 after, +1.20, the two multiplications by the gain. They were meant to run while 1/rms was made, but the jump left DVE nothing of that time: block 0's 1/rms was ready at 1360.87, 0.8 ahead of the first of them. The run with the old scaling: -1.18.

I had them beside other work because I looked at when they could start by their data, not at when DVE would reach them. The square sum's 0.4 us went nowhere, since it lies ahead of 1/rms.

**The start (-2.1, measured -1.82 in the profile, -1.6 in the run with both edits, whose interval is -0.3 to -2.7).** The mechanism was half right. The clock stayed full behind the zero products, but they lasted to 9.45 instead of 7.7. By (8.35 - 46 x 0.107) / 0.1065 about 32 of the 46 records were slow and not 16. (The granted clock reads 1.00 from the start on, but four to seven records in each microsecond up to 7.0 are those of half clock; there the spacing tells and not the column.) That the first weight product came only at 9.64 is also an accident of this execution: ACT waited for its input until 7.00, and until 5.90 in the run with 8 and 4 zero products, which starts with the same code. There the first weight product came at 8.55 and the Fourier stage at 31.02, as forecast. That the 23 products alone would be worth most of it is not borne out: alone they gave 0.0, with PE waiting 1.7 us for DVE's `pt_lo` in the Fourier stage. The prediction says "DVE comes last there", but charged it 0.1.

**The pairs (-0.8, measured -0.80)** and **the moved split (+1.5, measured +1.57)** were right in size and mechanism. The split's delay stood in DVE's row as computed (2.2 us more behind `xg_lo`), and taking it out gave 1.5 back. The rival on it, that DVE reaches it during the gather's products, failed as argued. **The gates (-0.1, measured -0.25):** the wait of 0.4 in step 1 went and one of 0.3 came ahead of the last hid.

Of the signs to look for, four came, one of them roughly: the Fourier stage near 31.1 (31.70), no wait for `used`, a wait of 1.0 us in the second up piece, a wait ahead of the last hid. The first weight product came at 9.64 and not near 8.65, with ACT's first high half at 7.00 and not 6.01. The first output issue, forecast 0.7 later relative to the last hid, came 1363.70 - 1345.85 - (1360.77 - 1345.53) = 2.6 later.

## What to carry to other kernels

Zero products that hold the clock are on the path as soon as what they wait for can come sooner: give them the length of the gap, and read it again each time the work ahead gets shorter. Work that is moved is priced in the row of its engine, with everything between the place and the next wait, a taken jump included, and not by when its data are ready. Where the clock falls and rises at other moments in each execution, look at the spread of the executions before explaining a microsecond of a median.

## What the runs showed of the chip

**Code behind a taken jump.** In all fifteen kernels that have the jump DVE's first operation behind it starts 2.95 to 3.26 us after PE's last scatter product ends, though block 0's 1/rms was ready 0.6 us before it in the kernel before, 0.8 us in the changed one. In the two kernels where DVE falls through, it starts 0.04 us after 1/rms in one and 0.04 us after the last sum in the other. That the wait comes with the jump is shown by these two; what in the jump takes the time, such as the fetch of instructions, no run shows.

**POOL beside DVE.** A one-column step of POOL took 0.27 us with DVE idle and 1.11 us with DVE's two multiplications of two operands running; the power that ends 1/rms took 0.58 alone and 1.03 beside the scaling, both in the kernel before. That DVE causes it is read from the overlap of these rows; no run moves DVE's work alone, though the run with the old end has the 0.27 again. The Trainium skill ("SBUF — State Buffer", SBUF: two separate sides) says that a DVE operation with two operands in SBUF and a POOL operation that reads SBUF exclude each other for their whole length. The end at 1352.6 of both agrees. In the changed kernel DVE came so late that POOL was undisturbed.

**The clock.** In the changed kernel it fell to half at 386 to 388, with PE busy 1.48 of 2.00 us and no gap over 0.6 us, and came back amid the zero products (0.75 between 392 and 394, 1.00 from 394). In the run with the old final scaling, with the same code up to there, it was 1.00 until 388 and again from 392. This shift is worth 1.3 us at the rank product (394.93 and 396.24). Why it differs between executions stays open.
